# The opening of a two-model forward pass: loads in pieces, and the first norm's sum behind two blocks

## The chip, the cores and the metric

The kernel runs on one core of one Trainium2 chip. The time is the device time of one execution in microseconds (us); several runs are given by their median. Before the change three runs took 1633.09, 1632.76 and 1629.13 us: median 1632.76.

## The reference, cut to what matters

All is in float32. 16 meta tokens are put ahead of 256 tokens of width 1024 (272 columns), and pass through two layers of a first model (norm, mixed attention, norm, MLP), then the 256 go through a second model (retention, block attention, two mixtures of experts). What the change touches is the very first step:

```
x = concat(meta_tokens, x)                       # 272 x 1024
r = 1 / sqrt(mean(x * x, axis=-1) + 1e-6)        # one number for each token
proj = (x * r * g) @ w_in_even                   # 1024 -> 2304
qa, ka, va, qb, kb, vb = split(proj)             # 512, 512, 512, 512, 128, 128 columns
```

kb and vb are one block of 128 columns each, qb four. Both qb and kb are then normalized by head and rotated; relrow is a table of relative-position biases, multiplied out from one-hot columns and written to DRAM, from where it is read back in shifted rows.

## The kernel before

Tokens lie in the free dimension, features in the 128 partitions: hT is 128 x 8 x 272, one chunk c of 128 features behind the other. To keep float32 accuracy at speed, each weight and each input is split into a high part (a rounding to a reduced format, by ScalarE) and a low part (the rest, by VectorE), and each product is taken in three passes (L1071 low weight x high input, L1072 high x low, L1073 high x high).

The norm's factor r isn't applied to the input: it is constant for a token, so the blocks are computed from x * g, and r is multiplied in where VectorE drains a block from PSUM (L2172, the drain or eviction). So r is wanted at the first drain and not at the first product.

A weight tile is 2 MB, 128 x 8 x 512, loaded by SP in the order of LOADS (L948 to L961) into one of four ring slots. A quarter of it is one block of 128 columns. Tile one, ("in0", 4), holds kb and vb in its first two quarters; the last two are never read. ScalarE (`split_weights`, L1671, copy at L1682) and VectorE (L2095, subtraction at L2101) split quarter after quarter, up to three ahead of TensorE, into four buffers. Both keep to an order that is written out by hand for each engine, as do TensorE and GpSimd; every engine takes its instructions strictly in order, and semaphores tie them together.

The opening, by engine:
- SP: all tokens in one transfer (L948), gains, two matrices of constants ("ident" and "ones", L950), tile one, the table for relrow (L953, L954), tile two, more constants (L956), and further tiles as slots come free (L886).
- GpSimd: squares the eight chunks (L975), each with a count of its own; then it waits for relrow to write it out (L977) and read it back (L981).
- ScalarE: high parts of the input (L1735), `split_weights(1)`, the root of the norm (L1737, recorded at L1662), then the high parts of the next weights.
- VectorE: low parts of the input (`spread`, L2127), `split_weights(1)`, then it waits for the root and takes the reciprocal (L2157), `split_weights(3)`, the two evictions of relrow (L2160, L2161), and then low parts and drains in turn: kb, vb, qb0, qb1, ...
- TensorE: the sum of squares over features as eight products with a matrix of ones (L1118 to L1123), kb (L1202), relrow (L1206), vb (L1208), qb0 (L1209), the head sums of squares (L1128), qb1 and so on.

The planner (`plan_first_stage`, L246) gives each product its PSUM bank: blocks and small products take banks 6 and 7 in turn, relrow 3 and 4, the norm bank 5. A product waits until the bank's last user has been drained. Its `put` calls (L296 on) must stand in TensorE's order, since each takes the next count of the semaphore psum_full.

Of the kernel before, what the change touches and what calls it, by code (L numbers as in the profile page):

```python
# [33 lines left out]
ALU = mybir.AluOpType  # L34
# [3 lines left out]
P = 128  # L38
D = 1024
# [121 lines left out]
def program(nc, A, out, dbg=None):  # L161
# [5 lines left out]
    def sem(name):  # L167
        return ctx.enter_context(nc.semaphore(name))
# [77 lines left out]
    def plan_first_stage():  # L246
# [28 lines left out]
        def put(key, *banks):  # L275
            by, n = drained[key]
            if not banks:
                banks = (6 + two[0] % 2,)
                two[0] += 1
            plan(key, by, *banks, drained=n)  # L280

        def block(key):
            put(key)
            j, q = COLUMN0[key[0]]
            plan_quarter("in0", j, q + key[1], count["full"])
            uses[key]["quarter"] = len(quarters) - 1
# [6 lines left out]
            else:  # L293
                uses[key]["quarter"] = uses[key[0], n - 1]["quarter"]

        put(("norm", 0), 5)  # L296
        block(("kb", 0))
        put("relrow_a", 4)
        put("relrow_b", 3)
        block(("vb", 0))  # L300
        block(("qb", 0))
        put(("headsq", 4))
        block(("qb", 1))
# [219 lines left out]

    recent = list(range(DENSE_SLOTS))
    tile, loads, holder = {}, [0] * DENSE_SLOTS, [None] * DENSE_SLOTS
    mlp_slots = {}
# [74 lines left out]
    def const(name, *dims):  # L603
        a = cst[:, CONST[name][0]:CONST[name][1]]
        return a.rearrange("p (a b) -> p a b", a=dims[0]) if dims else a
# [171 lines left out]
    drained = {"act": act_drained, "dve": dve_drained, "sum": sum_drained}  # L777
    pool_squared, gate_scaled, both_summed = sem("pool_squared"), sem("gate_scaled"), sem("both_summed")
    w_full = [sem(f"w_full{s}") for s in range(DENSE_SLOTS)]
    x_loaded, const_loaded, small_loaded = sem("x_loaded"), sem("const_loaded"), sem("small_loaded")  # L780
    oneh_loaded, tables_loaded, gains_loaded = sem("oneh_loaded"), sem("tables_loaded"), sem("gains_loaded")
    relrow_ready, relrow_saved, bias_a_loaded, bias_c_loaded = (sem("relrow_ready"), sem("relrow_saved"),
# [95 lines left out]
    def _(sp):  # L878
        def load(key, pairs=None):
            t = tile[key]  # L880
            if t["after"] is not None:
                if t["after"][0] == "moe":
                    sp.wait_ge(moe[t["after"][1]]["pe"], pairs * 6 + pe_read[t["slot"] % 3])
                else:
                    sp.wait_ge(*tile_free(t["after"]))
            sp.dma_start(ring[:, t["slot"], :], A["w_dense"][t["n"], :, :]).then_inc(w_full[t["slot"]], 16)  # L886
# [58 lines left out]
        pe_read = {0: 6 - 6, 1: 7 - 6, 2: 11 - 6}  # L945
        pairs = None

        sp.dma_start(hT[:, :, :], A["x"][:, :, :]).then_inc(x_loaded, 16)  # L948
        sp.dma_start(gain[:, :], A["gains"][:, :]).then_inc(gains_loaded, 16)
        sp.dma_start(cst[:, 0:2 * P], A["constants"][:, 0:2 * P]).then_inc(const_loaded, 16)  # L950
        for key in LOADS:
            if key == ("in0", IN0[1]):
                sp.dma_start(onehot_table, A["rel_table"][:, :]).then_inc(oneh_loaded, 16)  # L953
                sp.dma_start(onehot[:, 0:NREL], A["onehot"][:, :]).then_inc(oneh_loaded, 16)  # L954
            if key == ("in0", IN0[2]):
                sp.dma_start(cst[:, 2 * P:late], A["constants"][:, 2 * P:late]).then_inc(tables_loaded, 16)  # L956
            if key[0].startswith("mlp"):
                if key[1] == 0:
                    load_mlp(int(key[0][-1]))
                continue  # L960
            load(key, pairs)  # L961
            if key == ("ret_out", 3):
                pairs = load_experts(0)
        load_experts(1)
# [5 lines left out]

    @block.gpsimd
    def _(pool):
        pool.wait_ge(x_loaded, 16)
        for c in range(KC):
            pool.tensor_tensor(xn[:, c, :], hT[:, c, :], hT[:, c, :], ALU.mult).then_inc(x_squared, 1)  # L975
        pool.wait_ge(relrow_ready, 1)
        pool.dma_start(A["scratch"][:, :], relrow[:, 0:NREL]).then_inc(relrow_saved, 16)  # L977
        pool.wait_ge(relrow_saved, 16)
# [74 lines left out]
    def _(pe):  # L1053
        def take(key):

            for e, n in uses[key]["before"].items():
                pe.wait_ge(drained[e], n)
            return psum[:, uses[key]["banks"][0], :] if len(uses[key].get("banks", [0])) == 1 else None
# [56 lines left out]
        KT = [(0, P), (P, 2 * P), (2 * P, T0)]  # L1115
        QT = [(META, META + P), (META + P, T0), (0, META)]

        pe.wait_ge(const_loaded, 16)  # L1118
        o = take(("norm", 0))
        for c in range(KC):  # L1120
            pe.wait_ge(x_squared, c + 1)
            mm = pe.matmul(o[:, 0:T0], const("ones"), xn[:, c, :], start=(c == 0), stop=(c == KC - 1))
        mm.then_inc(psum_full, 1)  # L1123

        def heads_square(n):
            o = take(("headsq", n))
            pe.wait_ge(headsq_ready, 1 if n == 4 else n + 2)
# [76 lines left out]
        for key, a, b in (("relrow_a", 0, 512), ("relrow_b", 512, NREL)):  # L1204
            o = take(key)
            pe.matmul(o[0:A_HEADS + C_HEADS, 0:b - a], onehot_table, onehot[:, a:b], start=True,  # L1206
                      stop=True).then_inc(psum_full, 1)
        columns(("vb", 0), xh, xl, T0)  # L1208
        columns(("qb", 0), xh, xl, T0)  # L1209
        pe.wait_ge(tables_loaded, 16)  # L1210
        heads_square(4)
# [434 lines left out]
    def _(act):  # L1646
# [24 lines left out]
        def split_weights(upto, last_down=None):  # L1671

            while done[0] < min(upto, segment_end[segment[0]]):
                c = done[0]
                name, j, q = quarters[c]
                t = tile[name, j]
                act.wait_ge(w_full[t["slot"]], 16 * t["load"])
                if c >= 4:
                    act.wait_ge(psum_full, read[c - 4])
                if c == segment_end[0]:  # L1680
                    act.wait_ge(moe[0]["pe"], last_down)
                act.activation(split_view(wh, (name, j), c), quarter_view((name, j), q), ACT.Copy).then_inc(wh_ready, 1)  # L1682
                done[0] += 1
# [46 lines left out]
        act.wait_ge(eps_set, 1)  # L1730
        act.activation(warm, eps[:, 0:1], ACT.Sqrt)
        act.wait_ge(gains_loaded, 16)
        act.wait_ge(x_loaded, 16)
        for c in range(KC):
            act.activation(xh[:, c, :], hT[:, c, :], ACT.Copy, scale=gain[:, c:c + 1]).then_inc(xh_ready, 1)  # L1735
        split_weights(1)
        drain(("norm", 0), rms[:, 0, :], lambda o: o[:, 0:T0], ACT.Sqrt, bias=eps[:, 0:1], scale=1.0 / D)  # L1737
        KT = [(0, P), (P, 2 * P), (2 * P, T0)]
        QT = [(META, META + P), (META + P, T0), (0, META)]

# [7 lines left out]
        def values_turned(j):  # L1748
# [2 lines left out]
            act.activation(dst[:, 0:2, :], o[:, 0:2 * P].rearrange("p (k d) -> p k d", k=2), ACT.Copy)  # L1751
            act.activation(dst[0:META, 2, :], o[0:META, 2 * P:3 * P], ACT.Copy).then_inc(act_drained, 1)

        split_weights(AHEAD)
        stay_ahead(("vb", 0))
        square_heads(4)
# [319 lines left out]
    def _(v):  # L2076
# [13 lines left out]
        def drained_by_act(key):  # L2090
            v.wait_ge(act_drained, uses[key]["drained"])
# [28 lines left out]
                                       scalar=gain[:, 8 * g + c:8 * g + c + 1], in1=rms[:, 1, 0:T],  # L2120
                                       op0=ALU.mult, op1=ALU.mult).then_inc(out_ready if i == 10 else xn_ready, 1)

        def spread(name, c0, T, g):

            for c in range(KC):
                v.wait_ge(xh_ready, split_base[name] + c + 1)
                v.scalar_tensor_tensor(out=xl[:, c, c0:c0 + T], in0=hT[:, c, c0:c0 + T],  # L2127
                                       scalar=gain[:, 8 * g + c:8 * g + c + 1], in1=xh[:, c, c0:c0 + T].bitcast(F32),
                                       op0=ALU.mult, op1=ALU.subtract).then_inc(xl_ready, 1)
# [21 lines left out]
        v.memset(eps[:, :], EPS).then_inc(eps_set, 1)  # L2151
        v.wait_ge(gains_loaded, 16)
        v.wait_ge(x_loaded, 16)
        spread("norm0", 0, T0, 0)
        split_weights(1)
        drained_by_act(("norm", 0))
        link(v.reciprocal(rms[:, 1, :], rms[:, 0, :]))  # L2157
        split_weights(AHEAD)
# [659 lines left out]
```

## Time and profile before

| | us |
|---|---|
| median of three runs | 1632.76 |
| the profiled execution | 1637.88 |
| its span | 1636.1 |
| TensorE busy in it | 1514.5 (93%) |
| VectorE busy | 817.0 (50%) |
| ScalarE busy | 594.7 (36%) |
| GpSimd busy | 181.2 (11%) |
| TensorE's first product of the norm | at 7.00 |
| its first product of kb | at 14.97 |

The span runs from the first to the last instruction of the program on the core; the profiled execution took 1.8 us beyond it. All times of day ("at 14.97") are from the start of the span. The profile gives the busy time of each engine, what ended each idle stretch, and the chain of work that ended last.

### The profile page before, as it was taken

How to read it: one execution, taken by the hardware profiler on the slowest of the kernel's cores; microseconds unless marked ns; L12 is line 12 of the kernel's file. 1: busy time of each engine (PE TensorE's matmuls, PEld its weight loads, DVE VectorE, ACT ScalarE, POOL GpSimd, SP SyncE). 2: the span in 40 equal slices, each digit the busy share in tenths (PEclk: the TensorE clock that was granted, in tenths of full speed). 3: DMA queues.
4: the chain of work that ended last, by engine and by line, in shares of the span. 5: the costliest groups of instructions: out<-in, count | busy, mean ns of one | idle time of the engine just before them, and what ended most of it. 6: DMA issues, size and time to landing. Idle time of an engine off the chain costs nothing.

```text
span 1636.1 us, 25272 instructions
## 1 busy us (share of the span) xinstructions
PE 1514.5 (93%) x9938; PEld 1164.3 (71%) x9938; DVE 817.0 (50%) x1435; ACT 594.7 (36%) x1032; POOL 181.2 (11%) x171
## 2 busy tenths in 40 slices
PE   7998899998989999889989899999898989999997
PEld 6775899997679999888989754544657864444544
DVE  6867666676766666685566421111545441111213
ACT  4565544434654444534444211111424421111111
POOL 1000522253004332300000000000200000000000
PEclk9998999998999999989999899999999989999998
DMA  9041655444134545434511699999624169999993
GB/s 395 4 155 52 222 183 194 155 155 155 53 136 155 203 165 199 155 127 183 205 53 59 256 418 429 428 429 428 273 103 155 52 260 425 429 428 428 428 429 122
DMA packets 28753, 379.66 MB, mean 232 GB/s; under 512 B 3446, under 2 KB 4854, under 8 KB 5760
## 3 DMA queue, kind: packets, MB, share of 16 engines
q1 hardware_dynamic: 27312, 373.92, 57.3%
q0 software_dynamic: 928, 4.30, 0.7%
q8 instruction: 55, 0.90, 0.2%
q10 hardware_dynamic: 432, 0.32, 0.1%
q14 instruction: 26, 0.21, 0.0%
HBM read 377.45 MB, written 1.09 MB: 231 GB/s over the span
## 4 chain that ended last, share of the span: by engine, by line
PE 67%; DMA 16%; DVE 9%; ACT 3%; POOL 2%; issue 2%; SPq 0%; DVEq 0%; ACTq 0%; POOLq 0%
DMA ring<-w_expert_dram 15%; PE psum L1535 13%; PE psum L1071 13%; PE psum L1073 12%; PE psum L1072 12%; PE psum L1528 2%; PE psum L1093 2%; DVE weight_low L2101 2%; PE psum L1517 1%; POOL xn L1019 1%; PE psum L1428 1%; PE psum L1426 1%; PE psum L1427 1%; PE psum L1358 1%; PE psum L1348 1%
## 5 line engine op out<-in xcount | busy, mean ns | idle before, releaser
L1071 PE MATMUL psum<-x_high,weight_low 128*128 128x256 f32 (+1 forms) x1248 | 371.0, 297 | 32.9 <-DVE weight_low L2101 12.7
L1072 PE MATMUL psum<-x_low,weight_high 128*128 128x256 f32 (+1 forms) x1248 | 361.5, 290 | 0.0
L1073 PE MATMUL psum<-x_high,weight_high 128*128 128x256 f32 (+1 forms) x1248 | 361.5, 290 | 0.0
L2101 DVE TENSOR_TENSOR weight_low<-ring,weight_high 128x1024 fp32r<-128x1024 f32 x196 | 257.5, 1323 | 124.9 <-ACT weight_high L1682 124.4
L1535 PE MATMUL psum<-ring,xn 128*64 128x512 f32 x1152 | 263.2, 612 | 20.2 <-DMA ring<-w_expert_dram 19.8
L1071 PEld LDWEIGHTS psum<-x_high,weight_low 128*128 128x128 f32 x1248 | 242.8, 195 | 49.2 <-issue 21.7
L1682 ACT ACTIVATE weight_high<-ring 128x1024 fp32r<-128x1024 f32 x196 | 205.2, 1053 | 152.2 <-PE psum L1073 126.3
L1072 PEld LDWEIGHTS psum<-x_low,weight_high 128*128 128x128 f32 x1248 | 242.5, 194 | 1.7 <-issue 1.2
L1073 PEld LDWEIGHTS psum<-x_high,weight_high 128*128 128x128 f32 x1248 | 243.2, 195 | 0.0
L1535 PEld LDWEIGHTS psum<-ring,xn 128*64 128x64 f32 x1152 | 91.6, 141 | 188.1 <-issue 188.1
L1071 PE MATMUL psum<-hidden_high,weight_low 128*128 128x272 f32 (+1 forms) x512 | 147.2, 287 | 2.8 <-DVE hidden_low L2323 2.8
L1072 PE MATMUL psum<-hidden_low,weight_high 128*128 128x272 f32 (+1 forms) x512 | 147.1, 287 | 0.0
L1073 PE MATMUL psum<-hidden_high,weight_high 128*128 128x272 f32 (+1 forms) x512 | 146.8, 287 | 0.0
L1535 PE MATMUL psum<-ring,arena 128*64 128x512 f32 x576 | 127.6, 595 | 0.0
L2662 DVE TENSOR_TENSOR arena<-arena,psum 128x512 f32<-128x512 f32 x18 | 12.4, 687 | 227.5 <-PE psum L1535 227.5
L2315 DVE TENSOR_TENSOR weight_low<-ring,weight_high 128x1024 fp32r<-128x1024 f32 x64 | 87.1, 1361 | 60.7 <-ACT weight_high L1853 60.7
L1071 PEld LDWEIGHTS psum<-hidden_high,weight_low 128*128 128x128 f32 x512 | 97.7, 191 | 3.1 <-DVE hidden_low L2323 3.1
L1073 PEld LDWEIGHTS psum<-hidden_high,weight_high 128*128 128x128 f32 x512 | 98.0, 191 | 0.0
L1072 PEld LDWEIGHTS psum<-hidden_low,weight_high 128*128 128x128 f32 x512 | 97.8, 191 | 0.0
L1019 POOL TENSOR_TENSOR xn<-xn 128x256 f32<-128x256 f32 (+1 forms) x35 | 36.6, 1045 | 541.3 <-ACT xn L1716 537.0
L1535 PEld LDWEIGHTS psum<-ring,arena 128*64 128x64 f32 x576 | 39.7, 137 | 74.1 <-issue 72.0
L1853 ACT ACTIVATE weight_high<-ring 128x1024 fp32r<-128x1024 f32 x64 | 67.7, 1058 | 57.5 <-PE psum L1073 57.5
(339 smaller groups left out, 2114.3 us busy)
## 6 DMA issues: line engine op xcount, KB each, us to landing
ring<-w_expert_dram SPq DMA_DIRECT2D x108, 2048.0 KB, 16.0
ring<-w_dense_dram SPq DMA_DIRECT2D x68, 2048.0 KB, 8.2
arena<-scratch_dram POOLq DMA_DIRECT2D x1, 3328.0 KB, 12.8
constants_sb<-constants_dram SPq DMA_DIRECT2D x1, 1287.5 KB, 7.8
hT<-x_dram SPq DMA_DIRECT2D x1, 1088.0 KB, 5.2
constants_sb<-constants_dram SPq DMA_DIRECT2D x1, 1056.0 KB, 15.9
out_dram<-xn SPq DMA_DIRECT2D x8, 128.0 KB, 1.8
arena<-scratch_dram POOLq DMA_DIRECT2D x1, 832.0 KB, 14.2
```

Of the source, the lines that this page charges most:

```text
L1019: pool.tensor_tensor(part[:, 0, :], part[:, 0, :], part[:, c, :], ALU.add).then_inc(folded, 1)
L1071: pe.matmul(o, wl[:, c % 4, cols], high, start=start, stop=False)
L1072: pe.matmul(o, wh[:, c % 4, cols], low, start=False, stop=False)
L1073: return pe.matmul(o, wh[:, c % 4, cols], high, start=False, stop=stop)
L1093: mm = pe.matmul(o[0:b - a, 0:n], x[:, k, a:b], w[:, k, first:first + n], start=(k == 0), stop=(k == KC - 1))
L1348: mm = pe.transpose(psum[0:kb - ka, 4 + m, kt * P:kt * P + P], S1[:, s % 3, m, 1 + ka:1 + kb], const("ident"))
L1528: mm = pe.matmul(psum[:, c // 4, P * (c % 4):P * (c % 4) + P], xnat[:, tt, c * P:(c + 1) * P], oh[:, tt, :], start=(tt == 0), stop=(tt == 1))
L1535: mm = pe.matmul(psum[HALF * x:HALF * x + HALF, bank, :], x_[:, k, HALF * x:HALF * x + HALF], w[x][:, k, cols], start=start, stop=stop)
L1682: act.activation(split_view(wh, (name, j), c), quarter_view((name, j), q), ACT.Copy).then_inc(wh_ready, 1)
L1853: act.activation(split_view(wh, key, m["quarter"] + x), quarter_view(key, x % 4), ACT.Copy).then_inc(wh_ready, 1)
L2101: v.tensor_tensor(split_view(wl, (name, j), c), quarter_view((name, j), q), split_view(wh, (name, j), c).bitcast(F32), ALU.subtract).then_ ...
L2315: v.tensor_tensor(split_view(wl, key, c), quarter_view(key, x % 4), split_view(wh, key, c).bitcast(F32), ALU.subtract).then_inc(wl_ready, 1)
```

## The change

- SP loads the gains first, then the tokens in two halves of four chunks (the second half has a semaphore of its own, rest_loaded), then of tile one only the two used quarters, each a transfer of 128 x 8 runs of 512 bytes with its own semaphore (w_full and second_loaded), and then the constants.
- GpSimd adds the squares up itself: behind each square from the second on, an addition into chunk 0. TensorE's eight products with ones become one.
- TensorE takes this one product behind kb, relrow and vb, ahead of qb0; the planner's `put(("norm", 0), 5)` moves likewise.
- ScalarE splits the first weight quarter between the input's chunks 3 and 4, and the second ahead of the root.
- VectorE takes the low parts of chunks 0 to 3, of weight quarter one, of chunks 4 to 7 and of weight quarter two, and only then waits for the root.

```diff
-        put(("norm", 0), 5)
         block(("kb", 0))
         put("relrow_a", 4)
         put("relrow_b", 3)
         block(("vb", 0))
+        put(("norm", 0), 5)
         block(("qb", 0))
...
+    FIRST_TILE = ("in0", IN0[0])
...
-        sp.dma_start(hT[:, :, :], A["x"][:, :, :]).then_inc(x_loaded, 16)
         sp.dma_start(gain[:, :], A["gains"][:, :]).then_inc(gains_loaded, 16)
+        for a in (0, 4):
+            sp.dma_start(hT[:, a:a + 4, :], A["x"][:, a:a + 4, :]).then_inc(rest_loaded if a else x_loaded, 16)
+        t = tile[FIRST_TILE]
+        for q in range(2):
+            sp.dma_start(quarter_view(FIRST_TILE, q),
+                         A["w_dense"][t["n"], :, :].rearrange("p (k n) -> p k n", k=8)[:, :, P * q:P * q + P]
+                         ).then_inc(second_loaded if q else w_full[t["slot"]], 16)
...
-            load(key, pairs)
+            if key != FIRST_TILE:
+                load(key, pairs)
...
-        pool.wait_ge(x_loaded, 16)
         for c in range(KC):
+            pool.wait_ge(rest_loaded if c >= 4 else x_loaded, 16)
             pool.tensor_tensor(xn[:, c, :], hT[:, c, :], hT[:, c, :], ALU.mult).then_inc(x_squared, 1)
+            if c >= 1:
+                pool.wait_ge(x_squared, 2 * c)
+                pool.tensor_tensor(xn[:, 0, :], xn[:, 0, :], xn[:, c, :], ALU.add).then_inc(x_squared, 1)
...
-        pe.wait_ge(const_loaded, 16)
-        o = take(("norm", 0))
-        for c in range(KC):
-            pe.wait_ge(x_squared, c + 1)
-            mm = pe.matmul(o[:, 0:T0], const("ones"), xn[:, c, :], start=(c == 0), stop=(c == KC - 1))
-        mm.then_inc(psum_full, 1)
...
         columns(("vb", 0), xh, xl, T0)
+        pe.wait_ge(const_loaded, 16)
+        o = take(("norm", 0))
+        pe.wait_ge(x_squared, 2 * KC - 1)
+        pe.matmul(o[:, 0:T0], const("ones"), xn[:, 0, :], start=True, stop=True).then_inc(psum_full, 1)
         columns(("qb", 0), xh, xl, T0)
...
+                if (name, j) == FIRST_TILE and q == 1:
+                    act.wait_ge(second_loaded, 16)
...
-        act.wait_ge(x_loaded, 16)
         for c in range(KC):
+            if c % 4 == 0:
+                act.wait_ge(rest_loaded if c else x_loaded, 16)
+            if c == 4:
+                split_weights(1)
             act.activation(xh[:, c, :], hT[:, c, :], ACT.Copy, scale=gain[:, c:c + 1]).then_inc(xh_ready, 1)
-        split_weights(1)
-        drain(("norm", 0), rms[:, 0, :], lambda o: o[:, 0:T0], ACT.Sqrt, bias=eps[:, 0:1], scale=1.0 / D)
...
+        split_weights(2)
+        drain(("norm", 0), rms[:, 0, :], lambda o: o[:, 0:T0], ACT.Sqrt, bias=eps[:, 0:1], scale=1.0 / D)
         split_weights(AHEAD)
...
-        spread("norm0", 0, T0, 0)
+        spread("norm0", 0, T0, 0, range(4))
         split_weights(1)
+        v.wait_ge(rest_loaded, 16)
+        spread("norm0", 0, T0, 0, range(4, KC))
+        split_weights(2)
         drained_by_act(("norm", 0))
         link(v.reciprocal(rms[:, 1, :], rms[:, 0, :]))
         split_weights(AHEAD)
```

## Rows read from the trace of the kernel before

**Rows 1.** The page: engines' busy us, share, instructions; a DMA, KB, us to landing.
```profile
PE 1514.5 (93%) x9938; PEld 1164.3 (71%) x9938; DVE 817.0 (50%) x1435; ACT 594.7 (36%) x1032; POOL 181.2 (11%) x171
...
arena<-scratch_dram POOLq DMA_DIRECT2D x1, 3328.0 KB, 12.8
```

**Rows 2.** Chain of waits, 0 to 60 us: start, us, what.
```profile
12.61 1.07 ACT weight_high L1682
...
25.75 0.45 DVE arena L2172
...
26.56 0.48 ACT constants_sb L1662
27.06 1.86 DVE constants_sb L2177
...
54.16 1.86 DVE constants_sb L2177
```

**Rows 3.** Timeline of TensorE: start, us, line, out<-in, [idle before <-releaser].
```profile
14.97 0.40 PE L1071 MATMUL psum<-x_high,weight_low 128*128 128x272 f32 x1 [1.25 <-DVE weight_low L2101]
...
18.20 1.09 PE L1206 MATMUL psum<-arena 32*20 32x512 f32 x4
...
22.42 0.39 PE L1071 MATMUL psum<-x_high,weight_low 128*128 128x272 f32 x1
...
25.55 0.62 PE L1128 MATMUL psum<-xn,constants_sb 128*128 128x272 f32 x2
```

**Rows 4.** Timeline of VectorE: the opening, and low chunks at 175 us.
```profile
7.14 5.69 DVE L2127 SCALAR_TENSOR_TENSOR x_low<-hT,gains_sb,x_high 128x272 fp32r<-128x272 f32 x8 [6.29 <-ACT x_high L1735]
...
14.84 1.85 DVE L2157 RECIPROCAL rms<-rms 128x272 f32<-128x272 f32 x1
...
18.73 1.23 DVE L2101 TENSOR_TENSOR weight_low<-ring,weight_high 128x1024 fp32r<-128x1024 f32 x1 [0.78 <-ACT weight_high L1682]
...
25.75 0.44 DVE L2172 TENSOR_TENSOR arena<-psum,rms 128x272 f32<-128x272 f32 x1 [0.71 <-PE psum L1073]
...
175.69 1.32 DVE L2127 SCALAR_TENSOR_TENSOR x_low<-hT,gains_sb,x_high 128x272 fp32r<-128x272 f32 x3
```

**Rows 5.** Timeline of SP's queue: its issues.
```profile
0.73 0.40 SPq L948 DMA_DIRECT2D hT<-x_dram  x1
1.18 0.42 SPq L949 DMA_DIRECT2D gains_sb<-gains_dram  x1
```

**Rows 6.** DMA issues, 0 to 120 us: KB each, median us to landing.
```profile
hT<-x_dram SPq DMA_DIRECT2D x1, 1088.0 KB, 5.2
...
arena<-scratch_dram POOLq DMA_DIRECT2D x1, 832.0 KB, 14.2
...
scratch_dram<-arena POOLq DMA_DIRECT2D x1, 42.4 KB, 5.9
```

**Rows 7.** DMA queues, 0 to 20 us, ScalarE's: packets, MB, share of 16 engines.
```profile
q10 hardware_dynamic: 432, 0.32, 5.0%
```

**Rows 8.** Timeline of ScalarE, 0 to 60 us.
```profile
6.47 3.41 ACT L1735 ACTIVATE x_high<-hT,gains_sb 128x272 fp32r<-128x272 f32 x8 [2.83 <-DMA gains_sb<-gains_dram]
```

**Rows 9.** TensorE's weight loads, 6.5 to 12.1 and 12.8 to 13.9: busy us, mean ns, idle.
```profile
L1122 PEld LDWEIGHTS psum<-xn,constants_sb 128*128 128x128 f32 x12 | 3.9, 332 | 8.2 <-DMA constants_sb<-constants_dram 7.0
...
L1122 PEld LDWEIGHTS psum<-xn,constants_sb 128*128 128x128 f32 x3 | 0.6, 206 | 0.2
```

**Rows 10.** Timeline of GpSimd: opening, the fold at 177, pairs at 190.
```profile
6.03 1.24 POOL L975 TENSOR_TENSOR xn<-hT 128x272 f32<-128x272 f32 x2 [5.60 <-DMA hT<-x_dram]
...
177.28 9.76 POOL L1019 TENSOR_TENSOR xn<-xn 128x272 f32<-128x272 f32 x7 [149.31 <-ACT xn L1716]
...
190.34 0.63 POOL L998 TENSOR_TENSOR arena<-arena 128x272 f32<-128x272 f32 x1 [2.18 <-DVE rms L2138]
...
191.79 0.64 POOL L998 TENSOR_TENSOR arena<-arena 128x272 f32<-128x272 f32 x1
```

**Rows 11.** Waits, 0 to 80 us: total us, times, longest.
```profile
ACT weight_high L1682 <- DMA ring<-w_dense_dram: 5.1, 2, 2.7
```

More of the change, by code:

```diff
@@ L779, in program @@
     w_full = [sem(f"w_full{s}") for s in range(DENSE_SLOTS)]
+    second_loaded, rest_loaded = sem("second_loaded"), sem("rest_loaded")
     x_loaded, const_loaded, small_loaded = sem("x_loaded"), sem("const_loaded"), sem("small_loaded")
@@ L2121, in norm, with spread @@
                                        op0=ALU.mult, op1=ALU.mult).then_inc(out_ready if i == 10 else xn_ready, 1)
-        def spread(name, c0, T, g):
-            for c in range(KC):
+        def spread(name, c0, T, g, chunks=range(KC)):
+            for c in chunks:
                 v.wait_ge(xh_ready, split_base[name] + c + 1)
```

## Prediction

> **What bounds the kernel now.** I read the page first: TensorE is busy 93% of the span and VectorE 50% [rows 1]. The change touches the first 26 us alone, so these averages decide nothing; what counts is how many microseconds the opening gives to, or takes from, all that is behind it. The chain of waits of the first 60 us comes next [rows 2]. Weight tile one has landed at 12.61, ScalarE takes its high part in 1.07, VectorE its low part, and TensorE's first three-pass product starts at 14.97 [rows 3]. From there TensorE runs kb, relrow, vb and qb0 almost without a gap. At 25.75 the chain leaves it and goes VectorE, ScalarE, VectorE: the drain of qb0, a root, a reciprocal. qb1 needs the bank of qb0 and can't start before that drain.
>
> So two times matter: when TensorE starts, and when VectorE is through with its list up to the drain of qb0. In VectorE's timeline [rows 4] that list begins with the norm's reciprocal at 14.84, which lies under TensorE's kb today. Behind it VectorE is idle for 0.78 us at 18.73 and for 0.71 at 25.75: it has 1.5 us of slack and hardly more.
>
> **The change part by part.**
>
> *Landing.* SP's issues come 0.45 us apart [rows 5]. The gains go first, so the first half of the tokens is issued at 1.18. All of x (1088 KB) took 5.2 us to land [rows 6]: 5.97. Tile one needed 6.64 us more, in which it, the constants, the gains and some of ScalarE's loads moved, about 2.5 MB: 380 GB/s. Half of x is 1.4 us less at that rate, so it lands at 1.18 + 5.2 - 1.4 = 5.0, the other half near 6.4 (issued 0.45 later than x today). A quarter is 512 KB in 1024 runs of 512 B, a form that this trace doesn't have. The near end is the same rate, with 0.1 MB of ScalarE's queue beside it: 1.6 us, so 8.0. It can't be under that, as a run has no negative price. Next stand the small packets of ScalarE's queue: 432 take 5.0% of 16 engines over 20 us [rows 7], 37 ns each; 64 on each engine are 2.4 us, a landing at 9.0 with ScalarE's share. The far end is the strided read of the bias table, 2048 runs in 12.8 us [rows 1]: 6.3 ns a run, 6.4 us for 1024, a landing at 12.8. I take 8.4, between the near two, since the runs of the far one are longer and came from another queue.
>
> *Start of TensorE.* High part, low part and hand-overs took 14.97 - 12.61 = 2.4 us [rows 2, 3]: it starts at 10.8. The first four chunks are split before that: ScalarE's take 0.43 each (3.41 for 8) [rows 8], VectorE's 0.71 (5.69 for 8) [rows 4], the last of them done near 8.7. The other four low chunks follow low part one, 0.8 each, until 14; kb reads them one by one, at the lower clock no faster than they come.
>
> *TensorE comes in slow.* Today the norm's eight products (16 records) stand ahead of kb. In them a weight load takes 332 ns up to 12.1 and 206 behind 12.8 [rows 9]: the engine ran at the lower of its two levels (1.2 GHz) for some 5.6 us, busy from 7.0 on, and then at the upper (2.4 GHz). These products were hidden under the wait for tile one. In the changed kernel kb is TensorE's first work after idleness. Half speed over 3.4 to 5.6 us, the shorter end if it begins to count earlier than today, costs 1.7 to 2.8; I take 2.4.
> The profile's clock column says full speed for this stretch. The Trainium skill, "TensorE: Matmul & The Clock Gate", section "Part 1: The HAM clock gate", says that an idle TensorE is throttled and activity releases it. By that rule, with which the weight loads agree, kb pays; by the column it doesn't and the sum is 2.4 us smaller.
>
> *Up to the norm.* kb, relrow and vb take 22.42 - 14.97 = 7.45 at full speed, and a plain product over 272 columns, as in headsq, 0.65 [rows 3]: 8.1. TensorE is through with the norm at 10.8 + 2.4 + 8.1 = 21.3.
>
> *The fold on GpSimd.* Squares alone come 0.6 apart; a square and an operation that waits for it are a pair of 1.45 (190.34 to 191.79) [rows 10]. 0.6 + 7 x 1.45 = 10.75, from 5.0: 15.8 at the earliest. Beside VectorE's low parts of weights an addition takes 1.4 on average (7 in 9.76), 0.7 more than half such a pair; two of these meetings and 0.1 for each of eight low chunks give 18.0. vb ends on TensorE at 20.6, which covers the fold by 2.6 us; past that, each microsecond would count in full.
> The Trainium skill, "SBUF — State Buffer", section "SBUF: two separate sides", says that GpSimd and a VectorE operation with two SBUF inputs exclude each other for a whole instruction. The row of the low chunks disagrees in size: 0.71 a chunk beside the squares, where 0.6 and the 0.42 of a low chunk alone (three in 1.32 at 175 us) [rows 4] would be 1.02 in turn. By the rows the fold costs nothing; by the rule in full it has its rival below.
>
> *What is late next.* VectorE reaches its wait for the norm near 15.5 and stands there, with everything queued behind it: the reciprocal, the low part for qb0, relrow's two evictions, the low part for qb1, the drain of kb, two more low parts with the drain of vb, the drain of qb0. ScalarE's high parts from the third on stand behind the root likewise; at 1.05 each they keep ahead of VectorE. The root takes 0.5 with 0.1 of hand-over [rows 2], the reciprocal 1.88 with its hand-over, the rest of the list 25.75 - 18.73 = 7.0 less its idle 0.71 and 0.1: 6.2 [rows 4]. 21.3 + 0.6 + 1.9 + 6.2 = 30.0, where today it is 25.75: **4.2 us later**. TensorE idles meanwhile from 21.3 to 25 for qb0's low part, and before qb1 again.
>
> *Nothing:* the 1 MB of tile one that isn't loaded, since ScalarE waits for a weight tile twice in 80 us [rows 11], and the second wait ends at 17.6, before the norm now. Nor SP's three further issues (1.4 us), as tile two is wanted at 22. relrow is saved 4 us later; 5.9 + 14.2 us to the bias table [rows 6] end near 46, and VectorE asks for it behind 53: 7 us of cover.
>
> *To the end.* Behind 25.75 the chain stays between VectorE and ScalarE (27.06, 54.16) [rows 2] and no transfer ends a wait there, so I carry the delay whole.
>
> **Sum.** The profiled execution took 1637.88 us, 1.8 above its span; by it the changed one takes 1642.1. It stood 5.1 above the median of the three runs, 1632.76; to that I add the same 4.2: **1637.0 us**.
>
> One floor speaks against any gain. At full speed from its first product, a start S of TensorE leads to the drain of qb0 at S + 8.1 + 0.6 + 1.9 + 6.2 = S + 16.8. To equal 25.75, S must be 8.95 and the quarter in place at 6.55, with all of x queued ahead of it until 6.4.
>
> **Rivals.**
> 1. *The earlier start carries through.* If VectorE's list isn't on the path, the start 4.2 us earlier stands: 1628.6. For it: TensorE leads the chain until 25.75. Against it: the bank of qb1, and 6.2 us of list with 1.5 of slack.
> 2. *Break-even.* The quarter lands at 8.0 or before, TensorE is slow for 2 us only: +2.8, and slack further down takes that back: 1632.8. For it: the slow stretch is known from one case. Against it: no idle time of VectorE in the chain.
> 3. *Late pieces.* The 1024 runs cost more, up to the far end. At a landing of 11, midway to it, all is 2.6 later: +6.8, 1639.6. It passes 4.9 from a landing at 9.1 on. For it: the strided read. Against it: 37 ns a packet.
> 4. *Late fold.* With full exclusion, eight low chunks (0.42) and two low parts (1.14) add 5.6: the fold ends at 5.0 + 16.4 = 21.4 instead of under vb, the norm is 0.8 later: +5.0, 1637.8. It decides from 20.6 on. For it: 9.76 us at 177. Against it: 0.71. (The rule is that of the SBUF page of the Trainium skill, above.)
>
> **How the numbers follow.** A difference under 0.3% (4.9 us) can't be told from none here. Chances: forecast 0.62, rivals 0.10, 0.10, 0.11, 0.07. The forecast's own range is +1.5 to +6 (landing 8.0 to 9.0, the slow stretch 3.4 to 5.6, a share absorbed): 1634.3 to 1638.8; a third of it lies over 4.9. Slower: 0.21 + 0.10 + 0.04 = 0.35; faster 0.05, half of rival 1; the same 0.60. The range for 8 in 10 leaves out rival 1 and the far part of rival 3: 1631.0 to 1640.5.
>
> **What would show it.** TensorE's first three-pass product near 10.8; weight loads of some 330 ns in it, 190 in vb; GpSimd's last addition near 18, ahead of vb's last product; VectorE idle from 15.5 to 21.9, ended by ScalarE's root; qb0's first product near 25 and its drain near 30.0. A drain of qb0 before 25.8 makes the forecast wrong, and so does a drain at 30 in a kernel that takes no longer.

## The result and the profile after

The changed kernel takes 1640.63 us (median of 10, 1637.03 to 1644.91) where the kernel before takes 1632.77 (median of 10, 1629.13 to 1636.91). The ratio is 1.0052, 95% [1.0039, 1.0065]: slower by 6.4 to 10.6 us. The forecast was 1637.0, with 1631.0 to 1640.5 as its range. The direction held. The delay was forecast as 4.2 us and measured as 7.9, and the time lies just above the range: two steps behind the norm were missing from the sum. The profiled execution has a span of 1640.8 us, 4.7 above that of before.

The chain of waits of the first 66 us, by the columns of [rows 2], shows the new path through the opening.

```profile
2.11 7.18 DMA ring<-w_dense_dram
9.37 1.06 ACT weight_high L1693
...
12.25 0.60 PE psum L1083
...
22.70 0.50 ACT rms L1671
...
28.80 0.59 PE psum L1083
...
63.07 1.86 DVE constants_sb L2194
```

The drain of qb0 was at 25.75 and is at 34.65: 8.9 us later. The reciprocal that was at 54.16 [rows 2] is at 63.07: 8.9 later too. So the opening's loss is carried whole to there, as forecast; only it was to be 4.2. The same stretch on VectorE, to be held against [rows 4]:

```profile
10.46 1.74 DVE L2115 TENSOR_TENSOR weight_low<-ring,weight_high 128x1024 fp32r<-128x1024 f32 x1 [0.68 <-ACT weight_high L1693]
12.12 3.52 DVE L2141 SCALAR_TENSOR_TENSOR x_low<-hT,gains_sb,x_high 128x272 fp32r<-128x272 f32 x4
15.56 1.66 DVE L2115 TENSOR_TENSOR weight_low<-ring,weight_high 128x1024 fp32r<-128x1024 f32 x1
23.22 1.85 DVE L2174 RECIPROCAL rms<-rms 128x272 f32<-128x272 f32 x1 [6.00 <-ACT rms L1671]
25.11 1.23 DVE L2115 TENSOR_TENSOR weight_low<-ring,weight_high 128x1024 fp32r<-128x1024 f32 x1
...
28.31 0.43 DVE L2189 TENSOR_TENSOR arena<-psum,rms 128x272 f32<-128x272 f32 x1
...
30.19 1.23 DVE L2115 TENSOR_TENSOR weight_low<-ring,weight_high 128x1024 fp32r<-128x1024 f32 x1
34.65 0.44 DVE L2189 TENSOR_TENSOR arena<-psum,rms 128x272 f32<-128x272 f32 x1 [3.23 <-PE psum L1085]
```

The wait of 6.00 us for the root is the forecast one (15.5 to 21.9 there, 17.2 to 23.2 here). The last line is not: VectorE has run through its list by 31.4 and then stands idle for 3.23 us until qb0's last product. TensorE's waits and its table of stretches say why. First, of the waits of 0 to 60 us (line, releaser: total, times, longest), the one in question:

```profile
PE psum L1083 <- DVE arena L2189: 6.5, 2, 6.2
```

Then, for stretches bounded by hand, the length, the busy time (and instructions) of TensorE, its weight loads, VectorE, ScalarE and GpSimd, the granted clock, the DMA share and GB/s:

```profile
12.20:17.60 5.40, 5.35 (x23) 5.35 (x24) 5.02 (x5) 0.82 (x1) 5.17 (x6) 1.00 0.97 412
...
22.60:28.80 6.20, 0.00 (x1) 0.00 (x1) 5.40 (x7) 3.34 (x5) 0.74 (x1) 0.92 1.02 433
28.80:34.40 5.60, 5.60 (x24) 5.60 (x25) 2.62 (x3) 1.36 (x2) 0.73 (x1) 0.50 0.98 406
```

TensorE idles 6.20 us from 22.60 on. What ends that is not a low part of qb0's weights but L2189, the drain of kb: qb0 takes the PSUM bank that kb holds until 28.7. And behind the gap its 24 products take 5.60 us instead of the 3.2 of [rows 3], at a granted clock of 0.50, the lower level (1.2 GHz). kb, the first 24, takes as long (12.20 to 17.60), though the clock column says 1.00 there; its products come 0.23 us apart, where they come 0.13 apart at full speed. SP's issues and two of GpSimd's additions complete the picture:

```profile
2.11 1.47 SPq L955 DMA_DIRECT2D ring<-w_dense_dram  x2
3.62 3.72 SPq L958 DMA_DIRECT2D constants_sb<-constants_dram  x1
```

```profile
16.22 1.63 POOL L987 TENSOR_TENSOR xn<-xn 128x272 f32<-128x272 f32 x1
...
18.52 0.76 POOL L987 TENSOR_TENSOR xn<-xn 128x272 f32<-128x272 f32 x1
```

The first half of the tokens landed at 5.62 (forecast 5.0), quarter one at 9.37 (8.4). Behind the two quarters SP's next issue was held for 3.72 us. The fold ended at 19.3 (18.0), ahead of the norm's product at 21.98, so its end held nothing up. It wasn't free: beside it VectorE's first low part took 1.74 us instead of 1.24, and that one is on the path.

### The profile page after: what moved, and what is told of

The parts are those of the page before. It is cut to its first block, busy times and chain, and to the rows that moved or that the text cites. A ratio compares the mean times of both kernels' runs of the same rounds, so it can differ in the third digit from the quotient of the medians.

```text
span 1640.8 us, 25256 instructions
## 1 busy us (share of the span) xinstructions
PE 1507.1 (92%) x9924; PEld 1160.8 (71%) x9924; DVE 821.7 (50%) x1435; ACT 594.8 (36%) x1032; POOL 189.4 (12%) x178
## 4 chain that ended last, share of the span: by engine, by line
PE 67%; DMA 17%; DVE 9%; ACT 3%; POOL 2%; issue 2%; SPq 0%; DVEq 0%; ACTq 0%; POOLq 0%
DMA ring<-w_expert_dram 17%; PE psum L1083 13%; PE psum L1085 13%; PE psum L1084 12%; PE psum L1544 12%; PE psum L1537 2%; DVE weight_low L2115 2%; PE psum L1105 2%; PE psum L1526 1%; PE psum L1437 1%; PE psum L1435 1%; PE psum L1436 1%; PE psum L1367 1%; PE psum L1357 1%; PE psum L1159 1%
## 5 line engine op out<-in xcount | busy, mean ns | idle before, releaser
L1083 PEld LDWEIGHTS psum<-x_high,weight_low 128*128 128x128 f32 x1248 | 244.5, 196 | 66.7 <-DVE weight_low L2115 25.6
## 6 DMA issues: line engine op xcount, KB each, us to landing
constants_sb<-constants_dram SPq DMA_DIRECT2D x1, 1056.0 KB, 10.6
```

Source lines behind the costliest of these rows:

```text
L1083: pe.matmul(o, wl[:, c % 4, cols], high, start=start, stop=False)
```

## Experiments

The kernels leave nothing of the computation out. All were timed against the kernel before on the same chip. "Shift" is how much later than at 54.16 the same reciprocal comes in the experiment's trace; for the changed kernel it is +8.9. A trace is one execution, and its time lies up to 5 us from its kernel's median (before: 1637.88 for 1632.77), so I read shifts from the traces and whether a kernel is slower from the medians. There are 4 to 12 runs of each kernel. No timing separates bank, list_first, warm_gap or warm_open from the changed kernel, as their intervals overlap with its own; what a single step is worth rests on one trace for each.

### The order alone, the loads alone

*order_only*: the changed kernel with the old loads (tokens in one, then gains, constants and the whole of tile one).

```
-        for a in (0, 4):
-            sp.dma_start(hT[:, a:a + 4, :], ...)
-        ... two quarters of FIRST_TILE ...
+        sp.dma_start(hT[:, :, :], A["x"][:, :, :]); gains; constants; load(FIRST_TILE)
```

> The new order (norm behind vb, fold on GpSimd, VectorE's and ScalarE's new order) with the loads of before: x whole, tile one whole. Theory A (the order costs, in three steps: slow kb, the norm's list behind vb, qb0 held by the bank of kb and slow again): kb starts near 15.2, takes 5.6 us, the norm's product ends near 25.6, qb0 starts near 31.4 and is drained near 37.2, against 25.75 before: +11, median near 1644. Theory B (the 512-byte pieces cost, the order is harmless): qb0 is drained within 1 us of before, median within 2 us of before.

Measured (4 runs): 1642.28 against 1633.35, ratio 1.0072 [1.0046, 1.0099]; shift +11.1. TensorE and VectorE:

```profile
15.31 0.59 PE L1076 MATMUL psum<-x_high,weight_low 128*128 128x272 f32 x1 [15.31 <-DVE weight_low L2104]
...
31.23 0.60 PE L1076 MATMUL psum<-x_high,weight_low 128*128 128x272 f32 x1 [6.20 <-DVE arena L2175]
```

```profile
25.65 1.85 DVE L2160 RECIPROCAL rms<-rms 128x272 f32<-128x272 f32 x1 [8.69 <-ACT rms L1664]
...
36.81 0.44 DVE L2175 TENSOR_TENSOR arena<-psum,rms 128x272 f32<-128x272 f32 x1 [2.97 <-PE psum L1078]
```

The drain came at 36.81 where Theory A had 37.2. The new order alone does the whole damage. TensorE starts at 15.31, within 0.4 us of before, and the reciprocal that stood at 14.84 comes at 25.65. The new loads then give 2.2 us of it back.

*pieces_only*: the kernel before with the new loads (constants ahead of the tokens, so that the norm's eight products can still stand ahead of kb), no fold.

```
 sp.dma_start(gain...)  ; sp.dma_start(cst...)
+for a in (0, 4): sp.dma_start(hT[:, a:a + 4, :], A["x"][:, a:a + 4, :])
+for q in range(2): sp.dma_start(quarter_view(FIRST_TILE, q), ...[:, :, P * q:P * q + P])
```

> Only the loads in pieces and the splits that follow them; the norm stays eight products ahead of kb, and the two constant matrices are loaded ahead of the tokens. Theory A: the norm's products end near 13.2, kb follows at full speed at 13.2 instead of 14.97, qb0 starts near 20.7 and is drained near 24: 1.8 us sooner than before, median near 1631. Theory B: the pieces cost, quarter one lands at 9.3 or later and SP's queue is held for some 4 us, so that tile two is late: qb0 is drained at 26 or later, no gain.

Measured: 1633.64 against 1633.35, ratio 0.9999 [0.9985, 1.0013]; shift -0.1. Theory A's -1.8 missed; of Theory B the late quarter (10.12) and the held queue came, and its 26 for the drain was near. TensorE starts kb at full speed at 13.96, 1.0 earlier than before, but VectorE can't use it:

```profile
15.84 1.84 DVE L2174 RECIPROCAL rms<-rms 128x272 f32<-128x272 f32 x1
18.59 1.23 DVE L2115 TENSOR_TENSOR weight_low<-ring,weight_high 128x1024 fp32r<-128x1024 f32 x1 [0.92 <-ACT weight_high L1693]
...
21.80 0.43 DVE L2189 TENSOR_TENSOR arena<-psum,rms 128x272 f32<-128x272 f32 x1
...
25.60 0.44 DVE L2189 TENSOR_TENSOR arena<-psum,rms 128x272 f32<-128x272 f32 x1 [0.70 <-PE psum L1082]
```

```profile
17.43 2.96 ACT L1693 ACTIVATE weight_high<-ring 128x1024 fp32r<-128x1024 f32 x3 [2.52 <-DMA ring<-w_dense_dram]
```

ScalarE waits until 17.43 for tile two, and VectorE 0.92 us for ScalarE. Tile two landed hardly earlier than before (17.63), though 1 MB less stood ahead of it. Two things are in the trace. Its issue stood behind SP's held queue:

```profile
4.40 3.52 SPq L961 DMA_DIRECT2D arena<-rel_table_dram  x1
...
8.43 0.42 SPq L888 DMA_DIRECT2D ring<-w_dense_dram  x1
```

At the same time, while the pieces were on their way the DMA engines were as busy as before and moved fewer bytes. From 6 to 10 us, with DMA share and GB/s in the last two columns, in the kernel before:

```profile
6.00:10.00 4.00, 3.00 (x7) 2.30 (x8) 2.86 (x5) 3.41 (x8) 3.97 (x6) 1.00 1.08 445
```

And in pieces_only:

```profile
6.00:10.00 4.00, 2.56 (x6) 2.01 (x7) 2.66 (x4) 1.76 (x4) 3.35 (x5) 1.00 1.09 333
```

half_tile, below, takes the held queue away, and tile two gains only 0.7 us by it. So the held queue isn't the whole of it; that the lower rate is the rest is argued here and not shown. The smaller load by itself is worth nothing in any case, and qb0 starts at 22.29 where it started at 22.42.

### What the further 4.7 us are

*bank*: the changed kernel with qb0 in PSUM bank 0, which is free, instead of kb's.

```
-        block(("qb", 0))
+        block(("qb", 0), 0)
+        two[0] += 1
```

> The changed kernel with qb0 in PSUM bank 0 instead of bank 6, which kb still holds. Theory A (the bank holds qb0 from 26.3 to 28.8): qb0 starts at 26.4, as soon as its low part is there; it is drained at 32.1 if TensorE is slow after 3.7 us of idleness, or at 31.4, where VectorE's list ends, if it isn't; 34.65 in the changed kernel, so 2.5 to 3.3 us sooner. Theory B (the low part alone holds it): start stays at 28.8, drain at 34.65.

Measured: 1641.55 against 1633.35, ratio 1.0042 [1.0023, 1.0060]; shift +4.5. In the trace the drain of qb0 comes at 30.22, right at the end of VectorE's list, with no idle ahead of it:

```profile
12.11 0.60 PE L1084 MATMUL psum<-x_high,weight_low 128*128 128x272 f32 x1 [12.11 <-DVE weight_low L2116]
...
25.27 0.42 PE L1084 MATMUL psum<-x_high,weight_low 128*128 128x272 f32 x1 [3.78 <-DVE weight_low L2116]
```

```profile
22.11 1.85 DVE L2175 RECIPROCAL rms<-rms 128x272 f32<-128x272 f32 x1 [5.03 <-ACT rms L1672]
...
27.20 0.43 DVE L2190 TENSOR_TENSOR arena<-psum,rms 128x272 f32<-128x272 f32 x1
...
30.22 0.43 DVE L2190 TENSOR_TENSOR arena<-psum,rms 128x272 f32<-128x272 f32 x1
```

qb0 now waits for its low part and starts while kb still holds its own bank, ahead of the drain of kb at 27.20. Of the 4.4 us that the trace gains, 1.1 is not the bank's: the norm's sum was ready that much sooner in this execution (reciprocal at 22.11 for 23.22), because kb's products were slow only until 15.0 and took 4.6 us, where in the changed kernel's trace they were slow until 17.4 and took 5.6. The other 3.3 are the wait of 3.23. The 3.3 us rest on the trace, as said above.

*list_first*: the changed kernel with the low parts three and four and relrow's evictions ahead of the wait for the norm, instead of behind it, and ScalarE's high parts three and four ahead of the root. VectorE's part of the edit:

```
-        split_weights(2)
-        drained_by_act(("norm", 0))
-        link(v.reciprocal(rms[:, 1, :], rms[:, 0, :]))
         split_weights(AHEAD)
         ... relrow's two evictions ...
         stay_ahead(("kb", 0))
+        drained_by_act(("norm", 0))
+        link(v.reciprocal(rms[:, 1, :], rms[:, 0, :]))
         evict(("kb", 0))
```

> The changed kernel with the low parts (and high parts) of weights three and four and relrow's evictions ahead of the wait for the norm. Theory A (VectorE's list behind the reciprocal costs): reciprocal from 23.2 to 25.1 as before, kb drained at 25.5, qb0 starts at 25.6 instead of 28.8 and is drained at 28.9 if TensorE is still fast after 3 us of idleness, at 31.3 if not; 34.65 in the changed kernel. Theory B (the list was never on the path): no difference.

Measured: 1637.79 against 1633.35, ratio 1.0039 [1.0022, 1.0055]; shift +5.7. The reciprocal is where it was, and kb's drain stands right behind it:

```profile
23.24 1.85 DVE L2212 RECIPROCAL rms<-rms 128x272 f32<-128x272 f32 x1 [1.72 <-ACT rms L1671]
25.13 0.44 DVE L2185 TENSOR_TENSOR arena<-psum,rms 128x272 f32<-128x272 f32 x1
...
31.47 0.44 DVE L2185 TENSOR_TENSOR arena<-psum,rms 128x272 f32<-128x272 f32 x1 [3.23 <-PE psum L1085]
```

qb0's stretch, by the columns of the table of stretches above:

```profile
25.60:31.40 5.80, 5.78 (x25) 5.78 (x26) 2.64 (x3) 1.38 (x2) 0.81 (x1) 0.50 0.99 421
```

The drain of kb moves from 28.31 to 25.13, TensorE's gap from 6.2 to 3.0 us, and qb0's drain from 34.65 to 31.47: 3.2 each time, one for one. qb0's low part was ready by 19.5 here, so only kb's bank can have held qb0 from 22.6 until 25.6. Behind this gap of 3.0 us qb0 ran at 0.50 throughout; in bank, behind 3.8 us, its stretch from 25.4 to 29.9 had a mean of 0.62. So the length of the gap alone doesn't give the price.

*warm_gap*: the changed kernel with twelve products, in a bank that is free then, behind the norm's product, so that TensorE isn't idle while it waits.

```
+        for i in range(12):
+            pe.matmul(psum[:, 1, 0:T0], hT[:, 0, 0:P], hT[:, 1, :], start=True, stop=True)
         columns(("qb", 0), xh, xl, T0)
```

> The changed kernel with twelve products that nothing reads, taken by TensorE behind the norm's one, in its idle stretch from 22.6 to 28.8. Theory A (qb0 is slow because TensorE idled for 6.2 us before it): qb0 starts at 28.8 as before and takes 3.2 us instead of 5.6, its drain comes at 32.2 instead of 34.65. Theory B (qb0 is slow for another reason, such as contention with VectorE or with the loads): it still takes 5.6 us.

Measured: 1640.59 against 1633.83, ratio 1.0039 [1.0022, 1.0056]; shift +6.6.

```profile
22.63 5.66 PE L1134 MATMUL psum<-hT 128*128 128x272 f32 x24
28.99 0.39 PE L1083 MATMUL psum<-x_high,weight_low 128*128 128x272 f32 x1 [0.70 <-DVE arena L2196]
```

```profile
32.32 0.44 DVE L2196 TENSOR_TENSOR arena<-psum,rms 128x272 f32<-128x272 f32 x1 [0.70 <-PE psum L1085]
```

qb0 starts at the same time and runs at full speed: drain at 32.32 instead of 34.65. The 0.70 left is the bank's part once the clock's is gone. So the two missed steps are not a sum: with both, VectorE waits 3.23 us; without the clock's 0.70; without the bank's none in the trace of bank, where part of qb0 ran at full speed. At the lower clock throughout it would have ended near 25.3 + 5.6 = 30.9, 0.7 behind the end of the list.

*warm_open*: the same for the first slow stretch, nine such products ahead of kb, from when the first half of the tokens is there.

```
+        pe.wait_ge(x_loaded, 16)
+        keep_busy(9)
         columns(("kb", 0), xh, xl, T0, "norm0")
```

> The changed kernel with nine products that nothing reads ahead of kb, from the landing of the first half of the tokens (5.6) on. Theory A: kb starts at 12.25 as before but takes 3.3 us instead of 5.6; vb ends at 19.8, just behind the fold (19.3); the norm is done at 20.4 instead of 22.6, and qb0's drain comes 2.2 us sooner, near 32.4. Theory B (the fold or the low chunks, 0.8 us each, bound kb): kb ends at 16.3 or later and the fold holds the norm, so less than 1 us is won.

Measured: 1639.92 against 1633.83, ratio 1.0031 [1.0017, 1.0045]; shift +7.1. TensorE's busy time of the nine, and VectorE's two marks:

```profile
5.63 7.41 PE L1134 MATMUL psum<-hT 128*128 128x272 f32 x18 [5.63 <-DMA hT<-x_dram]
```

```profile
21.72 1.85 DVE L2182 RECIPROCAL rms<-rms 128x272 f32<-128x272 f32 x1 [4.45 <-ACT rms L1679]
...
32.82 0.44 DVE L2197 TENSOR_TENSOR arena<-psum,rms 128x272 f32<-128x272 f32 x1 [2.91 <-PE psum L1085]
```

kb then takes 3.7 us instead of 5.6 (0.2 of it a wait for a low chunk). Of these 1.9 us, 1.5 came through (reciprocal 21.72 for 23.22): the nine products ran slow themselves, and kb waited for them until 12.67 where it had started at 12.25. Theory A's 2.2 us was too much.

### Can it be mended?

*all_three*: warm_open, bank and list_first together.

> The changed kernel with three remedies at once: nine unread products ahead of kb, qb0 in bank 0, and the low parts three and four and relrow's evictions ahead of the wait for the norm. Theory A (these three are the whole loss): norm done at 20.4, qb0 starts there, the reciprocal ends at 22.9, the drain of qb0 comes at 25.9 against 25.75 before and 34.65 in the changed kernel; the median is that of before within 2 us. Theory B (something else costs, down the line): the drain comes at 25.9 and the median stays some us above before.

Measured: 1635.07 against 1633.83, ratio 1.0010 [0.9996, 1.0024]; shift +2.7. This one is separated from the changed kernel. TensorE's norm product and its later wait, and VectorE's drain of qb0:

```profile
20.93 0.70 PE L1226 MATMUL psum<-xn,constants_sb 128*128 128x272 f32 x2 [0.57 <-POOL xn L988]
...
32.40 0.99 PE L1140 MATMUL psum<-xn,constants_sb 128*128 128x272 f32 x2 [2.19 <-DVE arena L2194]
```

```profile
27.16 0.43 DVE L2194 TENSOR_TENSOR arena<-psum,rms 128x272 f32<-128x272 f32 x1
```

```profile
32.40:36.00 3.60, 3.60 (x14) 3.02 (x15) 1.96 (x2) 2.26 (x5) 0.00 (x0) 0.54 1.02 415
```

Theory A had the norm done at 20.4 and the drain of qb0 at 25.9; they came at 21.6 and 27.16. The fold has become the bound: TensorE waits 0.57 us for GpSimd's last addition. At qb0's drain the three repairs take back 7.5 of the 8.9 us. But at 54 us the shift is 2.7, not 1.4: the other 1.3 us are lost in between, where TensorE idles for 2.19 us ahead of 32.40 and the products behind that run at the lower clock, 0.54 in the mean until 36.0. Here the delay isn't carried whole; it grows by a third slow stretch. The changed order still isn't ahead of the old one.

*half_tile*: pieces_only, but the used half of tile one in one transfer (1024 runs of 1 KB for two times 1024 runs of 512 B).

```
-        for q in range(2):
-            sp.dma_start(quarter_view(FIRST_TILE, q), ...[:, :, P * q:P * q + P])
+        sp.dma_start(slot(t["slot"])[:, :, 0:2 * P], ...[:, :, 0:2 * P])
```

> As pieces_only (norm's eight products ahead of kb, constants ahead of the tokens, tokens in halves), but the two used quarters of tile one as one transfer of 1024 runs of 1 KB instead of two of 1024 runs of 512 B. Theory A (SP's queue is held by the number of runs in flight; it was held for 3.5 us at its next issue in pieces_only): the hold is under 1.5 us, tile two lands near 15.5 instead of 17.4, kb starts at 13.9 again, and the drain of qb0 comes at 24.7 instead of 25.6. Theory B (the hold is one of bytes, or of the two transfers): hold and landing of tile two stay, drain at 25.6.

Measured: 1633.25 against 1633.83, ratio 1.0000 [0.9990, 1.0009]; shift -0.2. Theory A was right on the queue and wrong on what it brings: the drain came at 25.54 for 24.7. SP's next issue is held far less and tile two's own stands at 4.93 instead of 8.43, but it landed only at 16.7. The half of tile one landed at 11.6, so the first low part came at 12.70 and the reciprocal at 16.63:

```profile
3.29 1.11 SPq L960 DMA_DIRECT2D arena<-rel_table_dram  x1
```

```profile
12.70 1.23 DVE L2112 TENSOR_TENSOR weight_low<-ring,weight_high 128x1024 fp32r<-128x1024 f32 x1 [2.23 <-ACT weight_high L1690]
```

```profile
22.20 0.40 PE L1079 MATMUL psum<-x_high,weight_low 128*128 128x272 f32 x1 [0.71 <-DVE arena L2186]
```

From 12.70 to kb's drain VectorE has no more than 0.15 us of idle time, so an earlier tile two has nothing left to shorten; what starts the list is the landing of the half, for which VectorE stood idle 2.23 us. Behind the list TensorE waits 0.71 us for kb's drain.

*half_bank*: half_tile, with qb0 in bank 0 (the edit of bank).

> A version that might beat both: half_tile (old place of the norm, tokens in halves, the used half of tile one as runs of 1 KB) with qb0 in bank 0. Theory A (kb's drain holds qb0, then VectorE's list holds the drain of qb0): kb from 13.98 to 17.2, vb to 21.4, qb0 starts at 21.4 instead of 22.2, and is drained when VectorE's list is through, at 24.75 instead of 25.54; 1.0 us sooner than before, carried to the end: ratio near 0.9994, too little for the median to show. Theory B (something behind the drain bounds the stretch to 50 us, so nothing is carried): reciprocal near 49 us within 0.2 of before's.

Measured: 1631.88 (12 runs) against 1633.08, ratio 0.9993 [0.9982, 1.0004]; shift -1.1 (the reciprocal at 53.04).

```profile
16.52 1.85 DVE L2172 RECIPROCAL rms<-rms 128x272 f32<-128x272 f32 x1
...
24.64 0.43 DVE L2187 TENSOR_TENSOR arena<-psum,rms 128x272 f32<-128x272 f32 x1
```

The drain of qb0 is at 24.64 (expected 24.75, before 25.75) and TensorE has no gap from kb to qb0. The median is 1.2 us under that of before and the interval holds zero, from -2.9 to +0.7 us. It is the best of the nine, and a gain that this timing doesn't prove.

Shifts against times, all ten kernels. Each shift lies within the interval of its ratio (times 1633), as a delay carried whole from there would; the intervals are 3 to 9 us wide, so a microsecond gained or lost behind 54 us wouldn't show. From qb0's drain to 54 us nine of the ten traces keep their shift to 0.1 us; all_three is the exception.

| kernel | shift at 54 us | ratio, 95% |
|---|---|---|
| changed | +8.9 | 1.0052 [1.0039, 1.0065] |
| order_only | +11.1 | 1.0072 [1.0046, 1.0099] |
| bank | +4.5 | 1.0042 [1.0023, 1.0060] |
| list_first | +5.7 | 1.0039 [1.0022, 1.0055] |
| warm_gap | +6.6 | 1.0039 [1.0022, 1.0056] |
| warm_open | +7.1 | 1.0031 [1.0017, 1.0045] |
| all_three | +2.7 | 1.0010 [0.9996, 1.0024] |
| pieces_only | -0.1 | 0.9999 [0.9985, 1.0013] |
| half_tile | -0.2 | 1.0000 [0.9990, 1.0009] |
| half_bank | -1.1 | 0.9993 [0.9982, 1.0004] |

## Why the prediction was right in its direction and wrong in two steps

The drain of qb0 was forecast at 30.0 and came at 34.65. The 4.7 us between them, in the order of the forecast's steps:

- *Landing, and the start of TensorE* (forecast 8.4 and 10.8, measured 9.37 and 12.25). Mis-sized by 1.0 and 0.5 us. The quarter took 7.2 us from its issue, near the second of the two near ends (9.0). The low part took 1.74 us instead of 1.24, since GpSimd's fold now runs beside it; the forecast priced such meetings for GpSimd only and not for VectorE. (In all_three the same low part took 1.23, and the addition that it met took 1.85.)
- *TensorE comes in slow* (2.4). Right: kb took 5.6 us for 3.2, and warm_open brought it to 3.7. The forecast's lower end for the slow stretch, 3.4 us, stood on no row; the traces have 5.2 us in the changed kernel (12.25 to 17.4) and 2.9 in bank (12.11 to 15.0).
- *Up to the norm* (8.1 at full speed). Right: from 12.25 to 22.6 are 10.35, against 10.5 forecast with the slow stretch. So the norm was done 1.3 later than 21.3, all of it from the start.
- *The fold* (18.0). Mis-sized by 1.3 us: it ended at 19.3. vb was later by as much, so the cover was 2.7 us where 2.6 was said. all_three shows the fold as the bound once the rest is 1 us faster. Rival 4's full exclusion (21.4) did not come.
- *The root, the reciprocal, the list* (0.6, 1.9, 6.2). Right: 23.22 to 31.4 is 1.9 + 6.2 and a little.
- ***"TensorE idles meanwhile from 21.3 to 25 for qb0's low part."*** This step failed: the wait was ended by another thing than the one named, and later. qb0 needed kb's bank, and the drain of kb stands in VectorE's list behind that low part, relrow's evictions and another low part. TensorE idled until 28.8. It could be seen before: the drain of kb took 21.93 to 22.36 and qb0 started at 22.42, but vb's last product had started at 22.21, so the bank cost next to nothing then. I had named the bank for qb1 and not asked it for qb0. bank and list_first show it.
- ***The second slow stretch.*** Missing from the sum altogether. I wrote that TensorE would idle for 3.7 us and priced the products behind that gap at full speed, one paragraph after pricing an idle engine's at half. qb0 at the lower clock takes 5.6 us for 3.2; with TensorE kept busy in warm_gap the drain comes 2.3 us sooner. By the Trainium skill, "TensorE: Matmul & The Clock Gate", section "Part 1: The HAM clock gate", an idle engine is throttled: the trace agrees, at 0.50 behind gaps of 6.2 and 3.0 us, where qb0 behind the 0.70 us of warm_gap reads 1.00.
- The last two together are the 3.23 us for which VectorE waits. Either alone would be worth 0.7 to 0.9, an estimate from the traces: qb0 from 28.8 at full speed ends at 32.0 (measured, 32.3), and qb0 from 26.3 at half speed would end at 31.9, both beside a list that ends at 31.4, with some 0.25 us from the last product to the drain.
- *Nothing, and to the end.* Held: no wait on the path ended with tile two, SP's issues or the bias table, and 8.9 us of delay stood at 54 us, with 7.9 between the medians.

1.3 from the start and 3.3 from TensorE's wait are 4.6 of the 4.7 us. Had both missed steps been in the sum, it would have run: norm done 21.3, reciprocal through at 23.8, kb's drain 3.2 behind it (28.31 less 25.11) at 27.0, qb0's start 0.5 later, its slow products and hand-over 5.85 (28.80 to 34.65), drain at 33.3. That is +7.6, and the start's 1.3 make the rest. Of the rivals, 3 (late pieces) came nearest in time, +6.8, with the wrong cause: its landing at 11 was not the measured 9.4. Rival 2 is mis-added: 0.4 off the landing and 1.4 off the slow stretch leave +2.4, not +2.8.

What this leaves open: why kb's slow stretch was 2.9 us in one execution and 5.2 in another, and how much of bank's gain a timing would show. Its shift of +4.5 lies in its interval (3.8 to 9.8 us), near the low end.

## What to carry to other kernels

A reciprocal, a root or any long operation that lies under TensorE's work costs its whole length, and that of everything queued behind it on its engine, once its input becomes TensorE's last product: compute the earliest start at which moving it could break even, before anything else. When a step is delayed, ask of every product behind the delay for both its operands and its bank, and read in the trace which ended last and by how little. And when the sum opens a gap on TensorE as long as those here (2.2 to 6.2 us), price the products behind it at the lower clock as well as at full speed, since a bank wait and a slow stretch hide in each other's slack when taken one by one. Repairs open gaps of their own, as all_three did, so follow the delay beyond the first place where it shows.

## What the runs showed of the hardware

- SP's queue was held behind strided loads in small runs: the issue after two transfers of 1024 runs of 512 B took 3.72 us (3.52 in pieces_only), after one of 1024 runs of 1 KB 1.11 us, where [rows 5] have 0.4. The runs don't tell whether the number of runs or of transfers does it, as half_tile changes both.
- Loads in short runs moved fewer bytes at the same busy share: from 6 to 10 us 445 GB/s before, 320 in the changed kernel and 333 in pieces_only (512 B), 351 in half_tile (1 KB), at DMA shares of 1.02 to 1.13. A load of half the bytes brought the next tile's landing no nearer (17.43 for 17.63) or little (16.7).
- VectorE and GpSimd lengthen each other: a low part of weights took 1.74 and 1.66 us beside the fold and 1.23 alone; GpSimd's operations beside it took 1.63 for 0.84. The Trainium skill, "SBUF — State Buffer", section "SBUF: two separate sides", has such pairs in turn, one after the other. A low part and a square in turn would be 1.23 + 0.6 = 1.83, near to 1.74 and 1.66, and in all_three the low part took its 1.23 and the addition 1.85. So the trace agrees for these. For low chunks it agrees only in part: a low chunk and a square in turn would be 0.42 + 0.6 = 1.02, where the first eight took 0.87 each (3.47 and 3.52 for four).
- TensorE's granted clock reads 1.00 in kb's stretch, while 24 products took 5.4 us as they did at a reading of 0.50 later. At the start of this program the column can't be used; the spacing of equal products can.
